# Linear attention: the row norm's factors reach all partitions through device memory instead of through TensorE

## The reference, cut to what matters

```python
hn = rms_norm(h, norm_mix[0])          # h * rsqrt(mean(h*h) + eps) * gain, per token
q, k, v, r, zf, zb = split_cols(hn @ w_in, ...)   # zf and zb are 16 columns each
la_f = log_sigmoid(zf @ w_gate_f + b_gate_f) / 16
la_b = log_sigmoid(zb @ w_gate_b + b_gate_b) / 16
```

## Time and profile before

| | us |
|---|---|
| median of 3 runs | 890.17 |
| lowest and highest | 889.98, 890.87 |
| the profiled execution's own time | 890.14 |
| its span | 888.3 |

### The profile page before, as it was taken

How to read it: one execution, slowest core, us unless ns; L and a number is a source line. 1 busy time by engine, 2 the same in 40 slices (tenths; PEclk the granted TensorE clock), 3 DMA queues, 4 the chain that set the end, 5 groups by cost and what they waited for, 6 DMA issues and landing times.

```text
span 888.3 us, 12038 instructions
## 1 busy us (share of the span) xinstructions
PE 883.5 (99%) x4300; PEld 729.6 (82%) x4300; DVE 669.0 (75%) x1031; ACT 504.3 (57%) x822; POOL 73.4 (8%) x88
## 2 busy tenths in 40 slices
PE   9999999999999999999999999999999999999998
PEld 8988888888888888778888888888888888887777
DVE  6997698666746599997787666646779987779763
ACT  7656464444535576887564444443765445577581
POOL 0002010000000303111100000000010000115200
PEclk9999999999999999999999999999999999999999
DMA  9754578777767567433387666675687774757501
GB/s 340 264 179 169 210 259 300 241 267 244 251 216 237 189 229 244 145 99 115 126 292 276 244 244 250 243 238 166 231 300 253 245 243 154 291 171 250 185 27 48
DMA packets 83715, 192.67 MB, mean 217 GB/s; under 512 B 7172, under 2 KB 37252, under 8 KB 83656
## 3 DMA queue, kind: packets, MB, share of 16 engines
q1 hardware_dynamic: 82200, 188.11, 61.5%
q0 software_dynamic: 1024, 3.15, 1.1%
q10 hardware_dynamic: 432, 0.66, 0.2%
HBM read 174.32 MB, written 17.56 MB: 216 GB/s over the span
## 4 chain that ended last, share of the span: by engine, by line
PE 98%; ACT 1%; DMA 1%; DVE 0%; issue 0%; ACTq 0%
PE bank L1867 88%; PE bank L1905 3%; PE bank L2159 1%; PE bank L2185 1%; PE bank L2265 1%; PE bank L1920 1%; PE bank L2295 1%; DMA h<-x_dram 1%; PE bank L2170 0%; PE bank L2251 0%; PE bank L2071 0%; PE bank L2067 0%; PE bank L2145 0%; PE bank L1886 0%; PE bank L2275 0%; PE bank L2044 0%
## 5 line engine op out<-in xcount | busy, mean ns | idle before, releaser
L1130 DVE TENSOR_TENSOR wlo<-raw,whi 128x1024 fp32r<-128x1024 f32 x295 | 346.9, 1214 | 35.5 <-ACT whi L719 35.2
L719 ACT ACTIVATE whi<-raw 128x1024 fp32r<-128x1024 f32 x295 | 302.2, 1060 | 112.8 <-PE bank L1867 97.6
L1867 PE MATMUL bank<-whi,x_hi 128*128 128x512 f32 x560 | 152.2, 394 | 0.0
L1867 PE MATMUL bank<-wlo,x_hi 128*128 128x512 f32 x560 | 149.8, 389 | 0.0
L1867 PE MATMUL bank<-whi,x_lo 128*128 128x512 f32 x560 | 149.8, 389 | 0.0
L1867 PEld LDWEIGHTS bank<-wlo,x_hi 128*128 128x128 f32 x560 | 105.1, 188 | 22.2
L1867 PEld LDWEIGHTS bank<-whi,x_lo 128*128 128x128 f32 x560 | 105.1, 188 | 22.0
L1867 PEld LDWEIGHTS bank<-whi,x_hi 128*128 128x128 f32 x560 | 103.6, 188 | 22.3 <-issue 1.8
L1867 PE MATMUL bank<-whi,y_hi 128*128 128x512 f32 x396 | 107.5, 393 | 0.1
L1867 PE MATMUL bank<-whi,y_lo 128*128 128x512 f32 x396 | 106.1, 390 | 0.0
L1867 PE MATMUL bank<-wlo,y_hi 128*128 128x512 f32 x396 | 106.0, 389 | 0.0
(11 more groups left out here) (260 smaller groups left out, 886.4 us busy)
## 6 DMA issues: line engine op xcount, KB each, us to landing
raw<-stream_dram SPq DMA_DIRECT2D x295, 512.0 KB, 4.7
ffn_blocks<-ffn_blk SPq DMA_DIRECT2D x22, 256.0 KB, 2.2
ffn_land<-ffn_blocks SPq DMA_DIRECT2D x22, 256.0 KB, 4.4
residual_blocks<-h_blk SPq DMA_DIRECT2D x18, 256.0 KB, 2.0
h_land<-residual_blocks SPq DMA_DIRECT2D x18, 256.0 KB, 2.9
cv_blocks<-cv_blk SPq DMA_DIRECT2D x7, 256.0 KB, 3.6
cv_land<-cv_blocks SPq DMA_DIRECT2D x7, 256.0 KB, 4.3
h_blocks<-h_blk SPq DMA_DIRECT2D x3, 512.0 KB, 2.9
```

Of the source, the lines that this page charges most:

```text
L719: A(whi[:, u % RING, :], raw[:, u % SLOTS, :], ACT.Copy).then_inc(sem("w_hi"), 1)
L1130: V.tensor_tensor(wlo[:, u % SLOTS, :], raw[:, u % SLOTS, :], whi[:, u % RING, :].bitcast(F32), ALU.subtract).then_inc(sem("w_lo"), 1)
L1867: last = T.matmul(bank[pair + t][:, :], lhs[a][:, kt, t * P:(t + 1) * P], w[:, place(w, u), kk * NW:(kk + 1) * NW], start=part != 1 and k ...
```

## The change

GpSimd, after `row_norm(0)`, writes `rstd` as 256 single numbers to a new tensor `norm_factors` in device memory, waits for that, and reads the 1 KB back to all 128 partitions of `factor`. The two diagonals, the matmuls with ones, the copy of z and the copy of bank 4 go. DVE multiplies z straight from bank 6 by `factor`. `z_spread` stands ahead of unit 6 instead of unit 5, and DVE drives `split_to` to unit 8 before "zT" (it was 5) and to unit 9 before "z4" (it was 6).

```diff
 GLA_ORDER = {
     "pe": (
-        (4, "zT", 0), (5, "z4", 0), (7, "gates", 0), (16, "scores", 0),
+        (6, "z4", 0), (7, "gates", 0), (16, "scores", 0),
 ...
     "dve": (
-        (4, "zT", 0), (4, "tile", 1), (5, "z4", 0), (5, "gates", 0), ...
+        (7, "zT", 0), (4, "tile", 1), (8, "z4", 0), (5, "gates", 0), ...
 ...
+        f_dram = nc.dram_tensor("norm_factors", (1, SEQ), F32, kind="Internal").ap()
 ...
             row_norm(0)
+            pool.wait_ge(sem("rstd"), 1)
+            nc.gpsimd.dma_start(f_dram.rearrange("o (t p) -> p (o t)", p=P), rstd[:, 0, :], allow_slow_non_contiguous=True)\
+                .then_inc(sem("factors_out"), 16)
+            pool.wait_ge(sem("factors_out"), 16)
+            nc.gpsimd.dma_start(factor, f_dram.to_broadcast([P, SEQ])).then_inc(sem("factors_in"), 16)
 ...
-            V.memset(gtmp[:, 2, 0:P], 1.0).then_inc(sem("gla_diag"), 1)
 ...
                 if step == "zT":
-                    dve.wait_ge(sem("rstd"), 1)
-                    for t in range(TT):
-                        V.tensor_scalar(gtmp[:, t, 0:P], ident, rstd[:, 0, t:t + 1], None, ALU.mult)\
-                            .then_inc(sem("gla_diag"), 1)
-                    dve.wait_ge(sem("gla_diag"), 3)
                     dve.wait_ge(sem("gla_z_filled"), 1)
-                    V.tensor_copy(zT[0:64, :], bank[6][0:64, 0:SEQ]).then_inc(sem("gla_z"), 1)
-                    dve.wait_ge(sem("gla_factors"), 1)
-                    dve.wait_ge(sem("gla_z"), 1)
-                    V.tensor_tensor(zT[0:64, :], zT[0:64, :], bank[4][0:64, 0:SEQ], ALU.mult)
-                    V.tensor_copy(factor, bank[4][:, 0:SEQ]).then_inc(sem("gla_zT"), 1)
+                    dve.wait_ge(sem("factors_in"), 16)
+                    V.tensor_tensor(zT[0:64, :], bank[6][0:64, 0:SEQ], factor[0:64, :], ALU.mult).then_inc(sem("gla_zT"), 1)
 ...
-            def z_factors():
-
-                pe.wait_ge(sem("gla_diag"), 3)
-                claim(4)
-                for t in range(TT):
-                    last = T.matmul(bank[4][:, t * P:(t + 1) * P], gtmp[:, 2, 0:P],
-                                    gtmp[:, t, 0:P], start=True, stop=True)
-                last.then_inc(sem("gla_factors"), 1)
-                free[4] = ("gla_zT", 1)
```

More of the change, by code:

```diff
@@ L137 @@
     "dve": (
-        (4, "zT", 0), (4, "tile", 1), (5, "z4", 0), (5, "gates", 0), (7, "ln", 0), (7, "sums", 0), (7, "ln", 1), (7, "sums", 1),
+        (7, "zT", 0), (4, "tile", 1), (8, "z4", 0), (5, "gates", 0), (7, "ln", 0), (7, "sums", 0), (7, "ln", 1), (7, "sums", 1),
         (9, "tile", 2), (9, "cumulate", 0), (10, "cumulate", 1), (11, "far", 0), (11, "far", 1), (12, "scores", 0),
@@ L2083, in gla_beside @@
                         continue
-                    if step == "zT":
-                        z_factors()
-                    elif step == "z4":
+                    if step == "z4":
                         z_spread()
```

## The result

| | us |
|---|---|
| before, median of 5 runs | 890.52 |
| after, median of 5 runs | 901.19 (900.25 to 903.79) |
| ratio, with its 95% interval | 1.0124 (1.0113 to 1.0135) |
| profiled execution after: its own time, its span | 902.42, 900.6 |

The kernel is 1.2% slower. That is far above the predicted 890.4, and outside the range, which ended at 893.0.

What follows compares the result with a forecast made beforehand. PE bounds the kernel, busy 883.5 of 888.3 us. A 0.70 us wait ahead of `z_spread` less 0.45 of removed matmuls gives +0.25 on 890.14, so 890.4 us; range 889.5 to 893.0.

Steps and rivals of the forecast that it cites:

- What bounds the kernel, what is removed, when PE and DVE are ready: PE bounds; its four passes go, 0.45 us gained; PE reaches `z_spread` at 25.17, DVE is free at 21.96.
- The factors' landing: GpSimd's write and read-back after `rstd`: issued at 16.76, landing times 8.3 us in all, ends 6.1 and 10.0.
- L1: Time from issue to landing of GpSimd's write of the factors to device memory, taken as 3.8 us.
- L2: Time from issue to landing of GpSimd's read of the factors to all partitions, taken as 4.5 us.
- the slow rival: GpSimd's transfers queue behind SP's weight loads, landing in 5.1 and 6.1 us, 11.2 in all: +3.15, 893.3 us; chance 0.18.
- The fit of 2.0 us and 436 KB per us: Skill's GpSimd DMA cost, fixed part plus rate: about 4.3 us for the pair, no PE wait; set aside for the rows.
- L1 + L2 - 8.05: Net change in us once both landings exceed 7.6: PE's wait ahead of `z_spread` less the 0.45 gained; forecast +0.25.
- Hidden wholly: Rival: both landings take at most 7.6 us, PE does not wait ahead of `z_spread`, gain 0.45: 889.7 us; chance 0.30.
- the limit of 7.6: Largest sum in us of the write's and read's landings at which PE does not wait ahead of `z_spread`.
- Descriptors held up by DVE: Rival: GpSimd cannot issue the write before DVE's run of subtractions ends at 21.96: +5.45, 895.6 us; chance 0.03.
- A second wait at the scores: Rival: the 0.78 us of room ahead of the scores is misread: +0.79 instead of +0.25, 890.9; within a shared 0.47.
- SP's loads: Weight loads share the DMA engines with 129 KB more; ACT's splits run ahead to unit 11, so nothing waits for them.

Runs made afterwards that it cites:

- filler: Changed kernel plus 20 extra matmuls of zeros on PE ahead of the wait of `z_spread`; 900.09 us, ratio to before 1.0114.
- pieces_8: Changed kernel with a partition's two factors written as one piece of 8 bytes and DVE reading them in the new order; 898.36 us, ratio to before 1.0084.
- held: Changed kernel with SP waiting until the factors have been read back before it loads unit 9 and what follows; 897.81 us, ratio to before 1.0085.
- resumed: Changed kernel with 8-byte pieces and SP's loads held only until the write has landed; 894.19 us, ratio to before 1.0035.
- both: Changed kernel with 8-byte pieces and SP's loads held until the factors have been read back; 892.00 us, ratio to before 1.0016.
- beside: Kernel before plus the changed kernel's write and read on GpSimd's queue, with no other engine waiting for them; 890.35 us against 890.38, ratio 1.0001.
- held_alone: Kernel before with SP loading unit 9 and what follows only after DVE's copy in z4, about 25.7 us; 892.63 us, ratio 1.0023.
- rows_1k: Kernel before plus an unawaited write of 128 pieces of 1 KB and a read of one row to all partitions, on GpSimd's queue; 890.76 us.

## Why the prediction was wrong

**What bounds the kernel, what is removed, when PE and DVE are ready: right.** PE went through units 4 and 5 without a gap and its last matmul ended at 25.23 (predicted 25.17). DVE was idle from 21.9 (21.96). The four passes are gone.

**The factors' landing: the step that failed.** The prediction put L1 at 3.8 and L2 at 4.5, with 10.0 as the upper end of their sum; they were 10.72 and 6.49, in all 17.2. That is outside every case the prediction priced by the landings, the slow rival's 11.2 included. It took both from "the nearest rows", GpSimd's transfers in the last attention, and let size (shorter) and the full engines (longer) pull against each other. The runs showed what stands in its place.
- The write's own cost is 8.3 us with nothing beside it. This is from packing 256 pieces into 1 KB; spread by 64 bytes it is 2.0, and as 128 packed pieces of 8 bytes 3.5. No row of the kernel before has pieces that close together, so its rows could not bound this, and "256 pieces of 4 bytes" was worth more than a remark in the text. The last paragraph of the prediction named a much longer single-number write as what would prove it wrong, but no rival carried a price for it.
- The loads beside it add 2.4 (8.3 to 10.7; and 2.3 to 4.7 for the rows of 1 KB; 2.0 to 3.4 over all the runs that have a quiet counterpart), and about 1.5 to 3 to the read. The slow rival had this mechanism and a fair price for the read, 6.1 against 6.5, but it put the write's 5.1 down to the queue alone and got 11.2 where 17.2 was needed.

The Trainium skill, "DMA: Bandwidth & Descriptors", section "Specifications", gives 512 bytes as the least transfer for the full rate, as below that a DMA engine reads, modifies and writes. Had size alone decided, both 4-byte writes would have been slow; the runs have 8.3 packed and 1.9 spread, so size alone does not decide here; among packed pieces it still counts (3.5 for 8 bytes). The fit of 2.0 us and 436 KB per us that the prediction cited from the same page gives 2.0 and 2.3, and holds for quiet transfers whose pieces do not share one 1 KB (1.9 and 2.0 for 1 KB; 2.2, 2.3 and 2.5 for 128 KB). It fails for all those that share one (3.5 to 8.3), and under the loads (4.7 for the rows of 1 KB).

**The sum: the rule was right, one term was missing.** "L1 + L2 - 8.05" gives +9.16 with the landings of the changed kernel, and the wait less the matmuls is 9.68 - 0.45 = 9.23. The term that the prediction did not have is what follows the wait, +2.9: a PE that waited was then granted 1.2 GHz for the next 6 us, which is 2.64 of it by filler, and the spread's 0.27 is there at the full clock too. With the landings of each run and the excess of its spread and unit 6 over the 0.43 and 2.87 of before, the rule gives the growth of each span:

| run | L1 + L2 - 8.05 | clock, with the 0.27 | sum | span less 888.3 |
|---|---|---|---|---|
| changed kernel | 9.16 | 2.90 | 12.1 | 12.3 |
| pieces_8 | 6.07 | 2.26 | 8.3 | 9.0 |
| held | 4.66 | 2.06 | 6.7 | 7.0 |
| resumed | 1.89 | 1.77 | 3.7 | 4.1 |

The second column of numbers is read from the profiles and not forecast; 0.2 to 0.7 us of each span stays without a line.

**Hidden wholly: right as a mechanism.** In both, with L1 + L2 at 7.1, `z_spread` did not wait, as the limit of 7.6 says. **Descriptors held up by DVE: no.** The write's issue took 0.91 us instead of 0.5 to 0.8 but was not put off, though DVE's subtractions ran from 17.31. In held, where DVE subtracted without a gap too, the write's first packet came 1.5 us after the issue, so the 3.8 of the changed kernel are not DVE's. **A second wait at the scores: none** in the changed kernel. **SP's loads: right that nothing waited for them**, for a reason I had not seen: beside shows that they can be slowed to a third and less for 6 us. The margin is thin, as held_alone shows.

What stays open: what happens between the last packet of such a write and its landing, and why the read of one row took 5.0 once and 3.5 once in quiet stretches (1.3 of the 1.5 us lie ahead of the read's first packet; the slower one read what the packed 4-byte write had just written). The landings are of one profile each. The change with its pieces 64 bytes apart, the obvious repair, was not run. An estimate from rows_1k, where a write and a read beside the loads took 4.7 and 6.3, is +2.95 by the rule, and what the clock adds: slower than before as well.

## What to carry to other kernels

Before a broadcast goes through device memory, ask where its pieces land and not only how large they are: 256 numbers packed in 1 KB cost 8.3 us, the same numbers 64 bytes apart 2.0. Price a round trip at the moment it is made, with the engines' load in that stretch, and when no row shows a kind of access, do not let the nearest rows bound it from above. Where a saturated engine waits, add what its clock loses after the wait, and before holding other transfers back to make room, ask when their data are needed next: 5 us of hold decided between nothing and 2 us.

## What the runs showed of the hardware that was not expected

- Writes of 4 bytes side by side: 8.3 us from GpSimd's queue and 7.9 from SP's, 6.8 of it in both after the last packet that the profile has; 3.5 as pieces of 8 bytes; 2.0 when 64 bytes apart, 1.9 when 512 bytes apart.
- Such a write slows others: the loads beside it fell from 398 to 139 GB/s, to 100 in the run beside and to 57 in filler. 128 pieces of 1 KB in the same place left them at 408.
- One row read by 128 partitions took 3.5 and 5.0 us in quiet stretches, 128 different rows 2.2.
- PE's granted clock fell to 0.50 while it waited for 9.7 us and was back at 1.00 only after about 6 us of work. In resumed a wait of 2.6 us was enough: the clock was at 1.00 when PE went on at 27.6, and 0.58 and 0.57 over the next two stretches of 2 us.
